# Ones multiplied into a free PSUM bank where TensorE waits, at 15 places of a two-block transformer kernel

## The chip, the cores and the metric

The kernel runs on one core of one Trainium2 chip. The metric is the device time of one execution in microseconds (us). TensorE (PE) does the matmuls, VectorE (DVE) and ScalarE (ACT) the elementwise work, and SyncE (SP) starts the DMA transfers that bring the weights. TensorE's clock has two levels, 1.2 and 2.4 GHz; the profile shows the granted clock as a share of 2.4 GHz, so 1.00 is the upper level and 0.50 the lower.

## The reference

All arrays are float32, with 256 tokens of width 1024. A first block has two layers, each an FFN, a token mixer and a second FFN, and each of the three is followed by a layer norm. A second block has one layer of multi-head latent attention (MLA) and one of gated linear attention (GLA), with a second stream of 256 context tokens.

```
def layer_norm(x, g, b):
    mu = jnp.mean(xf, -1, keepdims=True)
    var = jnp.mean(jnp.square(xf - mu), -1, keepdims=True)
    return ((xf - mu) * lax.rsqrt(var + LN_EPS) * g + b)
...
for l in range(2):                                   # first block
    y = swiglu(modulate(x, ...), ffn_w13[l, 0], ffn_w2[l, 0]);  x = layer_norm(ALPHA * x + 0.5 * (1 + ..) * y, ...)
    y = token_mixer(modulate(x, ...), w_in[l], ...);            x = layer_norm(ALPHA * x + (1 + ..) * y, ...)
    y = swiglu(modulate(x, ...), ffn_w13[l, 1], ffn_w2[l, 1]);  x = layer_norm(ALPHA * x + 0.5 * (1 + ..) * y, ...)
...
# in token_mixer, the gated delta rule:
qa, ka, va = jnp.split(causal_conv_silu(qkv_a, gdn_conv), 3, axis=-1)
qa = l2norm(split_heads(qa)); ka = l2norm(split_heads(ka))      # l2norm(x) = x * rsqrt(sum(x * x) + eps)
...
for i in range(2):                                   # second block: i = 0 MLA, i = 1 GLA
    hx = rms_norm(x, norm_g[i]) * (1 + scx) + sx
    hc = rms_norm(ctx, norm_g[i]) * (1 + scc) + sc
    yc, yx = mla_mixer(hc, hx, ...) if i == 0 else gla_mixer(hc, hx, ...)
```

## The kernel before, in words

Everything stays in SBUF except the weights, which arrive in chunks of 128x2048 float32 in a ring of 8 places. Activations lie with their width on the partitions, in 8 tiles of 128x256 (width by tokens). Most matmuls are made of three: weights and activations are split into a rounded high part and a remainder of type fp32r, and high by high, low by high and high by low are added up in PSUM. Those take 128x256 operands of type fp32r. ScalarE makes the high part of a chunk, VectorE the low part (`low`), both ahead of use. Each engine's program is written out by hand in one fixed order, with waits on the three semaphores `tensor_done`, `scalar_done` and `vector_done`; no scheduler moves anything.

The modules are numbered by `m`: in each layer an FFN (m = 0, 3), a mixer (1, 4), an FFN (2, 5), then MLA (6) and GLA (7). The places the change touches on TensorE:

- `norm_sums(m)`, run after each of the six modules 0 to 5. It sums over the 1024 channels by multiplying with a table of ones (a 128x128 left operand of plain float32): first the sums for the mean (`mu`, four matmuls into PSUM bank 4), then, once ScalarE has squared the centred values (`sq`) and VectorE has added some of them in pairs (`sqfold`), the sums of the squares (`var`, six matmuls into bank 5). After that ScalarE makes 1/sqrt, VectorE scales (`xn`), and the tiles of the next module's high part `xhi` come out, four from ScalarE and then four from VectorE, each of which releases two matmuls. Then follow the pass low by high, and the pass with the remainders `xlo` (`xl`), which VectorE makes from `xa` and `xhi`. For the norm of m = 5 the next module is MLA, which begins with the context's tiles (`whi_xa`).
- `mixer(l)`: TensorE projects the chunks `WIN_FIRST = [12, 0, 1, 2, 3, 4]` into banks 1 to 6. VectorE convolves each half chunk out of PSUM (`conv`, one TENSOR_SCALAR and three SCALAR_TENSOR_TENSOR) and ScalarE applies silu. After the fifth of them (i = 4) TensorE forms the sums of squares for q and k (`l2`, six 128x256 matmuls with the table `blk` into banks 1 to 3); it needs ScalarE's squares `l2sq`, which need the sixth half chunk convolved. ScalarE then computes the roots from these sums (`l2e`, `ri`), prepares a chunk (`win_high(m, 7)`), loads a table and copies the gates of chunk i = 5 (`proj_read_a`, res<-ps), for which VectorE waits before the ninth half chunk. Later TensorE multiplies k by k (`kk`), which waits for VectorE's `kb` and `gb_read`.
- the end of `mla()`: `next_sums(6)` adds the last squares for the next rms norm into bank 6 (`ms2`). Then `gla()` starts with `unit` number 0, which waits before each of its 8 tiles k for VectorE's `xd` and ScalarE's `xc`.

The matmul helper `mm` is line 347 for all of them, a transpose line 350; on ScalarE nearly everything is line 1459, on VectorE tensor_tensor is line 2068.

Of the kernel before, what the change touches and what calls it, by code (L numbers as in the profile page):

```python
# [90 lines left out]
def build(nc, stream, cond_in, cols_in, tab_in, wg_in, xt_in, ct_in, out, spread, marks):  # L91
# [3 lines left out]
    with ExitStack() as ctx:  # L95
# [52 lines left out]
        def step(*key):  # L148

            return marks[key][1] if marks else 1  # L150

        def step_of(*key):

            return (signals[marks[key][0]], marks[key][1]) if marks else (vector_done, 1)
# [17 lines left out]
        def bank(b, lo=0, hi=512):  # L172
            return PS[:, b, lo:hi]

        def banks(b, n):

            return PS[:, :, :].rearrange("p b n -> p (b n)")[:, b * 512:b * 512 + n]
# [4 lines left out]
        def table(name, lo=0, n=None):  # L182
            a, m = TAB[name]
            return tab[:, a + lo:a + lo + (m - lo if n is None else n)]
# [5 lines left out]
        def tiles(ap, n):  # L190
            return ap.rearrange("p (t n) -> p t n", n=n)
# [11 lines left out]
        ones = table("ones", 0, 128)  # L203
# [137 lines left out]
        def _(eng):  # L341
# [4 lines left out]
            def mm(o, l, r, start, stop, free=False):  # L346
                last[0] = nc.tensor.matmul(o, l, r, start=start, stop=stop, skip_group_check=free)  # L347

            def turn(o, i, k=128):
                last[0] = nc.tensor.transpose(o, i, ident[0:k, 0:k])  # L350

            def row_tile(parity):


                if parity:
                    last[0].then_inc(tensor_done, 1)
                    done.named()
                    eng.wait_ge(tensor_done, done.count)
# [17 lines left out]
            def release():  # L376

                last[0].then_inc(tensor_done, 1)
                done.named("chunk", held[0])
                if held[0] + 1 < len(order) and order[held[0] + 1] == ("rounded",):  # L380
                    found["chunk", held[0] + 1] = found["chunk", held[0]]
# [95 lines left out]
            def norm_sums(m):  # L477

                if m == 0:
                    eng.wait_ge(tables_in, 16)  # L480
                eng.wait_ge(vector_done, step("fold", m))
                for t in range(2):
                    mm(bank(4, 0, 256), ones, tiles(ff_sq, 256)[:, t], t == 0, False)
                for t in range(6, KT):
                    eng.wait_ge(vector_done, step("res", m, t))
                    mm(bank(4, 0, 256), ones, tiles(ff_res, 256)[:, t], False, t == KT - 1)
                last[0].then_inc(tensor_done, 1)
                done.named("mu", m)
                for t in range(4):
                    eng.wait_ge(scalar_done, step("sq", m, t // 2))  # L490
                    mm(bank(5, 0, 256), ones, tiles(ff_sq, 256)[:, t], t == 0, False)
                for q in range(2, 4):
                    eng.wait_ge(vector_done, step("sqfold", m, q))
                    mm(bank(5, 0, 256), ones, tiles(ff_sq, 256)[:, 2 * q], False, q == 3)
                last[0].then_inc(tensor_done, 1)
                done.named("var", m)

            def mixer(l):
                m = 3 * l + 1
# [16 lines left out]
                def project_halves(o, both, ch, t):  # L516

                    (hi, lo), at_t = both, slice(P * t, P * t + P)
                    for k in range(KT):
                        if ch < 13:  # L520
                            mm(o, hi[:, k, at_t], xhi[:, k, :], k == 0, False)
                            mm(o, lo[:, k, at_t], xhi[:, k, :], False, False)
                            mm(o, hi[:, k, at_t], xlo[:, k, :], False, k == KT - 1)
                        else:
                            mm(o, xhi[:, k, at_t], hi[:, k, :], k == 0, False)
                            mm(o, xhi[:, k, at_t], lo[:, k, :], False, False)
                            mm(o, xlo[:, k, at_t], hi[:, k, :], False, k == KT - 1)

                def project_first(both):

                    hi, lo = both
                    for k in range(KT):
                        eng.wait_ge(*step_of("xh", m, k))
                        for t in range(2):
                            mm(bank(1, 256 * t, 256 * t + 256), hi[:, k, P * t:P * t + P], xhi[:, k, :], k == 0 and t == 0, False, free=True)
                    eng.wait_ge(vector_done, step("wlow", m, 0))
                    for k in range(KT):
                        for t in range(2):
                            mm(bank(1, 256 * t, 256 * t + 256), lo[:, k, P * t:P * t + P], xhi[:, k, :], False, False, free=True)
                    for k in range(KT):  # L540
                        eng.wait_ge(vector_done, step("xl", m, k))
                        for t in range(2):
                            mm(bank(1, 256 * t, 256 * t + 256), hi[:, k, P * t:P * t + P], xlo[:, k, :], False, k == KT - 1, free=True)

                def weight_halves(i, ch):

                    no = take_both("win", l, ch)
                    if i:
                        eng.wait_ge(vector_done, step("wlow", m, i))
                    return tiles(low[:, (no + 1) % RING, :], 256), tiles(low[:, no % RING, :], 256)  # L550
# [88 lines left out]
                for i, ch in enumerate(WIN_FIRST):  # L639
                    both = weight_halves(i, ch)  # L640
                    if i == 0:
                        project_first(both)
                    else:
                        for t in range(2):
                            project_halves(bank(1 + i, 256 * t, 256 * t + 256), both, ch, t)
                    release()
                    found["proj", m, i] = found["chunk", held[0]]
                    if i == 4:
                        for p in range(3):
                            eng.wait_ge(*step_of("proj_read", m, p))  # L650
                        eng.wait_ge(scalar_done, step("l2sq", m))
                        for t in range(6):
                            mm(banks(1, 1536)[:, 256 * t:256 * t + 256], blk, tiles(g_sq, 256)[:, t], True, True)
                        last[0].then_inc(tensor_done, 1)
                        done.named("l2", m)
# [15 lines left out]
                for h in [0, 2, 4, 1, 3, 5]:  # L671
                    if h == 1:
                        row_tile(1)
                    for c in range(2):
                        u = 2 * h + c
                        mm(banks(1, 1536)[:, P * u:P * u + P], head(K, h, c), head(g_kb, h, c), True, True)
# [3 lines left out]
                for h in [0, 2, 4, 1, 3, 5]:  # L680
                    if h == 1:
                        row_tile(1)
                    for c in range(2):
                        u = 2 * h + c
                        mm(banks(4, 1536)[:, P * u:P * u + P], head(K, h, c), head(Q, h, c), True, True)
# [80 lines left out]
                for h in [0, 2, 4, 1, 3, 5]:  # L766
                    if h == 1:
                        row_tile(1)
                    mm(bank(3, 64 * h, 64 * h + 64), head(g_kg, h), head(S, h), True, True)
# [68 lines left out]
            def mla():  # L838
# [306 lines left out]
                next_sums(6)  # L1145
                last[0].then_inc(tensor_done, 1)
                done.named("ms2", 7)

            def gla():
                m = 7  # L1150
# [256 lines left out]
            for l in range(DEPTH):  # L1407
                ffn(l, 0)
                norm_sums(3 * l)
                mixer(l)  # L1410
                norm_sums(3 * l + 1)
                ffn(l, 1)
                norm_sums(3 * l + 2)
            mla()
            gla()

# [1604 lines left out]
```

## Time and profile before

| | |
|---|---|
| median of 3 runs | 1774.16 us (1772.45 to 1776.2) |
| the profiled execution | 1776.33 us, its span 1774.3 us |
| mean granted TensorE clock | 0.988 |
| PE busy | 1686.1 us (95%), 13112 instructions |
| DVE busy | 1323.5 us (75%) |
| ACT busy | 777.0 us (44%) |
| DMA | 331.92 MB, 48% of the 16 engines' span |

The span is the time from the first to the last instruction; 2.0 us of the execution lie around it. A plain float32 matmul shows as two MATMUL records, an fp32r matmul as one. In a timeline row, a start and a length are given for a merged run of alike instructions, xN is the number of records, and in brackets stands how long the engine was idle before it and which work ended that idle time. The records of PE overlap a little, since matmuls are pipelined: the price of one is best read from the distance of starts.

### The profile page before, as it was taken

What the parts mean: (1) busy time and instruction counts of PE and PEld (TensorE: products, weight loads), DVE (VectorE), ACT (ScalarE), POOL (GpSimd) and SP (SyncE); (2) the same over time, 40 slices, a digit from 0 to 9 for tenths busy, and PEclk for the clock granted to TensorE, in tenths of its full rate; (3) what the DMA queues carried; (4) which work ended last, traced back from release to release, by engine and by line L of the source; (5) the groups of instructions that cost most, each with busy time, mean ns of one, the idle gap of its engine ahead of it and who ended that gap; (6) DMA issues with size and microseconds to landing.
All of it is one profiled execution on the core that took longest, in us unless ns stands there. A gap on an engine that the chain in (4) does not pass through costs nothing. (4 is left out here: it accounts for less than half of the span.)

```text
span 1774.3 us, 30736 instructions
## 1 busy us (share of the span) xinstructions
PE 1686.1 (95%) x13112; PEld 1512.1 (85%) x13112; DVE 1323.5 (75%) x1965; ACT 777.0 (44%) x997; POOL 6.3 (0%) x14
## 2 busy tenths in 40 slices
PE   2999989999999999999899999999999999999998
PEld 2999978888899989999798779999886555759898
DVE  7777788855877778998878557999767768567844
ACT  2433365323633354343753327343652345355354
POOL 0000000000000000000000000000000000000000
PEclk9999999999999999999999999999999999999999
DMA  9868536351577746885364435776153200223102
GB/s 390 340 270 305 207 108 246 133 202 63 203 305 285 282 180 271 321 316 198 119 227 155 179 128 207 273 279 229 48 213 143 95 34 15 107 95 143 48 24 96
DMA packets 48807, 331.92 MB, mean 187 GB/s; under 512 B 5256, under 2 KB 8480, under 8 KB 9376
## 3 DMA queue, kind: packets, MB, share of 16 engines
q1 hardware_dynamic: 47808, 326.79, 48.2%
q0 software_dynamic: 864, 3.17, 0.7%
q8 instruction: 104, 1.70, 0.4%
q14 instruction: 31, 0.25, 0.0%
HBM read 328.87 MB, written 1.07 MB: 186 GB/s over the span
## 5 line engine op out<-in xcount | busy, mean ns | idle before, releaser
L347 PE MATMUL ps<-xhi,low 128*128 128x256 f32 x2048 | 499.5, 283 | 4.2 <-ACT xhi L1459 4.2
L347 PEld LDWEIGHTS ps<-xhi,low 128*128 128x128 f32 x2048 | 360.5, 190 | 6.4 <-ACT xhi L1459 5.6
L347 PE MATMUL ps<-xhi,whi_wk 128*128 128x256 f32 x1072 | 298.5, 288 | 40.5 <-ACT xhi L1459 38.7
L347 PE MATMUL ps<-xlo,whi_wk 128*128 128x256 f32 x1072 | 291.5, 281 | 0.0
L1459 ACT ACTIVATE wk<-ps 128x256 f32<-128x256 f32 (+5 forms) x219 | 108.1, 503 | 386.8 <-PE ps L347 320.8
L1459 ACT ACTIVATE whi_wk<-ring 128x2048 fp32r<-128x2048 f32 x100 | 191.6, 1918 | 195.3 <-DMA ring<-in_stream_dram 145.2
L347 PEld LDWEIGHTS ps<-xhi,whi_wk 128*128 128x128 f32 x1072 | 203.5, 195 | 43.2 <-issue 41.8
L2068 DVE TENSOR_TENSOR low<-ring,whi_wk 128x2048 fp32r<-128x2048 f32 (+1 forms) x101 | 228.4, 2264 | 6.6 <-ACT whi_wk L1459 6.6
L347 PE MATMUL ps<-wk 64*64 64x64 f32 (+10 forms) x2712 | 210.3, 262 | 5.8 <-ACT wk L1459 4.3
L347 PEld LDWEIGHTS ps<-wk 64*64 64x64 f32 (+4 forms) x2712 | 162.3, 146 | 55.0 <-issue 29.5
L347 PEld LDWEIGHTS ps<-xlo,whi_wk 128*128 128x128 f32 x1072 | 197.9, 189 | 0.0
L347 PE MATMUL ps<-hhi,low 128*128 128x256 f32 x704 | 196.8, 280 | 0.0
L2083 DVE CUSTOM_DVE_ANT_0 ring<-ring,cond,cols 128x1024 f32<-128x1024 f32 x144 | 178.3, 1278 | 11.0 <-DMA cols<-in_cols_dram 10.9
L1459 ACT ACTIVATE wk<-wk 128x256 f32<-128x256 f32 (+9 forms) x154 | 94.6, 643 | 200.9 <-DVE wk L2074 154.9
L347 PE MATMUL ps<-xa,ring 128*128 128x256 f32 (+1 forms) x608 | 146.0, 396 | 3.4 <-DVE xa L2071 3.1
L2068 DVE TENSOR_TENSOR wk<-wk,ps 128x256 f32<-128x256 f32 (+2 forms) x130 | 57.9, 462 | 122.1 <-ACT wk L1459 108.6
L347 PE MATMUL ps<-hhi,whi_wk 128*128 128x256 f32 x528 | 148.0, 280 | 0.0
L347 PE MATMUL ps<-hlo,whi_wk 128*128 128x256 f32 x528 | 147.9, 280 | 0.0
L347 PEld LDWEIGHTS ps<-xa,ring 128*128 128x128 f32 x608 | 114.3, 191 | 30.1 <-issue 11.5
L347 PEld LDWEIGHTS ps<-hhi,low 128*128 128x128 f32 x704 | 132.2, 188 | 0.0
L2068 DVE TENSOR_TENSOR low<-ring,low 128x2048 fp32r<-128x2048 f32 x41 | 93.2, 2286 | 48.4 <-ACT low L1459 48.2
L347 PE MATMUL ps<-wk,tab 128*128 128x256 f32 (+3 forms) x370 | 96.6, 422 | 22.8 <-ACT wk L1459 19.9
(141 smaller groups left out, 2861.7 us busy)
## 6 DMA issues: line engine op xcount, KB each, us to landing
ring<-in_stream_dram SPq DMA_DIRECT2D x302, 1024.0 KB, 5.7
ring<-in_cond_dram SPq DMA_DIRECT2D x4, 1024.0 KB, 4.6
wk<-spread_dram POOLq DMA_DIRECT2D x4, 384.0 KB, 5.1
wk<-spread_dram POOLq DMA_DIRECT2D x2, 768.0 KB, 6.9
tab<-in_tab_dram SPq DMA_DIRECT2D x1, 1440.0 KB, 20.5
res<-in_xt_dram SPq DMA_DIRECT2D x1, 1024.0 KB, 17.5
res<-in_ct_dram SPq DMA_DIRECT2D x1, 1024.0 KB, 9.9
out_dram<-wk SPq DMA_DIRECT2D x4, 256.0 KB, 2.4
```

The costliest lines, as they stand in the source:

```text
L347: last[0] = nc.tensor.matmul(o, l, r, start=start, stop=stop, skip_group_check=free)
L1459: return nc.scalar.activation(o, i, f, **kw)
L2068: return do(v.tensor_tensor(o, a, b, op), *key)
L2083: return do(v.tensor_tensor_reduce(o, w, c, 1.0, bias, MUL, ADD, total), *key)
```

## The change

A helper `idle(b, n)` issues n plain float32 matmuls of the table of ones (its first 128 columns the left operand, all 256 the right) into the first half of PSUM bank b, as one accumulation that nothing reads. It signals nothing and waits for nothing of its own. It is called with bank 0 everywhere:

- in `norm_sums`, 3 matmuls between the sums for the mean and those for the variance, and 4 after the latter: at six norms, 42 matmuls
- in `mixer`, 9 matmuls ahead of the sums of squares of q and k, behind the three waits for the banks (`proj_read` 0 to 2) and before the one for `l2sq`: in two mixers, 18
- at the end of `mla`, 6 matmuls after the last sums

Together these are 66 matmuls or 132 records, all on TensorE.

```
             def turn(o, i, k=128):
                 last[0] = nc.tensor.transpose(o, i, ident[0:k, 0:k])
+
+            def idle(b, n):
+
+                for i in range(n):
+                    mm(bank(b, 0, 256), ones, table("ones"), i == 0, i == n - 1)
...
                 last[0].then_inc(tensor_done, 1)
                 done.named("mu", m)
+                idle(0, 3)
                 for t in range(4):
                     eng.wait_ge(scalar_done, step("sq", m, t // 2))
...
                 last[0].then_inc(tensor_done, 1)
                 done.named("var", m)
+                idle(0, 4)
...
                         for p in range(3):
                             eng.wait_ge(*step_of("proj_read", m, p))
+                        idle(0, 9)
                         eng.wait_ge(scalar_done, step("l2sq", m))
...
                 next_sums(6)
                 last[0].then_inc(tensor_done, 1)
                 done.named("ms2", 7)
+                idle(0, 6)
```

The order of TensorE's instructions at a norm, that of m = 1 (before, and with + the new rows; `tab` holds the ones, `wk` the squares and sums, `xhi` the next module's tiles):

```order
 L347 MATMUL ps<-wk,tab 128x256
 L347 MATMUL ps<-wk,tab 128x256 [waits vector_done] x2
+L347 MATMUL ps<-tab 128x256 x3
 L347 MATMUL ps<-wk,tab 128x256 [waits scalar_done] x4
 L347 MATMUL ps<-wk,tab 128x256 [waits vector_done] x2
+L347 MATMUL ps<-tab 128x256 x4
 L347 MATMUL ps<-xhi,whi_wk 128x256 [waits scalar_done,chunk_landed_6]
 L347 MATMUL ps<-xhi,whi_wk 128x256
```

Three matmuls now stand ahead of the first one that waits for ScalarE's squares, and four ahead of the first one that waits for `xhi`; nothing else has another place.

And in the mixer of m = 1, at the sums of squares of q and k (`wk` with `tab`), between the projections (`xhi`, `xlo`):

```order
 L347 MATMUL ps<-xhi,low 128x256 x2
 L347 MATMUL ps<-xlo,low 128x256
-L347 MATMUL ps<-wk,tab 128x256 [waits vector_done,scalar_done]
+L347 MATMUL ps<-tab 128x256 [waits vector_done]
+L347 MATMUL ps<-tab 128x256 x8
+L347 MATMUL ps<-wk,tab 128x256 [waits scalar_done]
 L347 MATMUL ps<-wk,tab 128x256 x5
 L347 MATMUL ps<-xhi,low 128x256 [waits vector_done]
```

The wait for the PSUM banks has moved to the first of nine new matmuls; the wait for the squares stays where it was.

## Rows read from the trace of the kernel before

**Rows 1.** The page's busy times.
```profile
PE 1686.1 (95%) x13112; PEld 1512.1 (85%) x13112; DVE 1323.5 (75%) x1965; ACT 777.0 (44%) x997; POOL 6.3 (0%) x14
```

**Rows 2.** Stretches (start:end, length, busy by engine), ending in clock, DMA share, GB/s.
```profile
230.00:250.00 20.00, 17.89 (x130) 16.18 (x129) 14.70 (x31) 17.97 (x28) 0.00 (x0) 1.00 0.23 79
260.00:280.00 20.00, 14.76 (x94) 13.51 (x93) 18.77 (x33) 11.04 (x10) 3.12 (x5) 0.83 0.37 124
450.00:460.00 10.00, 9.05 (x59) 8.66 (x60) 9.89 (x22) 9.73 (x15) 0.00 (x0) 0.83 0.07 13
...
840.00:860.00 20.00, 16.45 (x106) 15.04 (x105) 14.26 (x32) 15.90 (x25) 0.00 (x0) 0.91 0.14 54
1260.00:1280.00 20.00, 17.98 (x103) 15.54 (x103) 11.34 (x18) 13.42 (x28) 0.00 (x0) 0.91 0.00 1
1570.00:1580.00 10.00, 7.99 (x16) 3.60 (x17) 7.49 (x16) 7.20 (x12) 0.00 (x0) 0.83 0.46 193
```

**Rows 3.** Timeline, TensorE, the norm of m = 0 and what follows.
```profile
228.76 2.95 PE L347 MATMUL ps<-wk,tab 128*128 128x256 f32 x12 [1.45 <-ACT wk L1459]
233.82 5.32 PE L347 MATMUL ps<-xhi,low 128*128 128x256 f32 x32 [2.11 <-ACT xhi L1459]
241.31 0.40 PE L347 MATMUL ps<-xhi,low 128*128 128x256 f32 x2
```

**Rows 4.** Timeline, TensorE, after the norms of m = 3, 1 and 4.
```profile
847.98 5.67 PE L347 MATMUL ps<-xhi,low 128*128 128x256 f32 x32 [2.11 <-ACT xhi L1459]
855.48 0.40 PE L347 MATMUL ps<-xhi,low 128*128 128x256 f32 x2
...
450.94 3.94 PE L347 MATMUL ps<-xhi,whi_wk 128*128 128x256 f32 x16 [2.20 <-ACT xhi L1459]
458.76 0.28 PE L347 MATMUL ps<-xhi,whi_wk 128*128 128x256 f32 x1
...
1065.17 3.94 PE L347 MATMUL ps<-xhi,whi_wk 128*128 128x256 f32 x16 [2.20 <-ACT xhi L1459]
1073.11 0.28 PE L347 MATMUL ps<-xhi,whi_wk 128*128 128x256 f32 x1
```

**Rows 5.** Timeline, TensorE, the start of MLA, after the norm of m = 5.
```profile
1263.03 1.89 PE L347 MATMUL ps<-whi_xa,low 128*128 128x256 f32 x8 [1.22 <-ACT whi_xa L1459]
1265.72 9.23 PE L347 MATMUL ps<-whi_xa,low 128*128 128x256 f32 x56 [0.80 <-ACT whi_xa L1459]
1274.78 3.62 PE L347 MATMUL ps<-wk,tab 128*128 128x256 f32 x16
1278.05 4.17 PE L347 MATMUL ps<-whi_xa,low 128*128 128x256 f32 x32
```

**Rows 6.** Timeline, TensorE and ScalarE, sums of squares in the mixer m = 1.
```profile
269.32 5.38 PE L347 MATMUL ps<-wk,tab 128*128 128x256 f32 x12 [5.24 <-ACT wk L1459]
274.22 0.72 PE L347 MATMUL ps<-xhi,low 128*128 128x256 f32 x2
...
274.74 1.55 ACT L1459 ACTIVATE wk<-ps,cols 128x1536 f32<-128x1536 f32 x1 [4.26 <-PE ps L347]
```

**Rows 7.** Timeline, VectorE: the wait for the gates in m = 1, `gb_read`, then m = 4.
```profile
281.40 0.48 DVE L2071 TENSOR_SCALAR wk<-ps,cols 128x256 f32<-128x256 f32 x1 [0.86 <-ACT res L1459]
289.93 1.76 DVE L2068 TENSOR_TENSOR wk<-wk,tab 128x1536 f32<-128x1536 f32 x1
...
895.64 0.48 DVE L2071 TENSOR_SCALAR wk<-ps,cols 128x256 f32<-128x256 f32 x1 [0.59 <-ACT res L1459]
```

**Rows 8.** Timeline, TensorE, the first matmuls of `kk` in the mixer m = 1.
```profile
291.87 5.92 PE L347 MATMUL ps<-wk 64*128 64x128 f32 x48
```

**Rows 9.** Timeline, TensorE and VectorE, the start of GLA.
```profile
1572.01 10.28 PE L347 MATMUL ps<-xa,ring 128*128 128x512 f32 x20 [3.14 <-DVE xa L2071]
...
1577.05 0.73 DVE L2071 TENSOR_SCALAR xa<-wk,aux,mod 128x256 f32<-128x256 f32 x2
```

**Rows 10.** Timeline, VectorE, a low half in the projections of MLA.
```profile
1327.19 2.29 DVE L2068 TENSOR_TENSOR low<-ring,low 128x2048 fp32r<-128x2048 f32 x1 [4.03 <-ACT low L1459]
```

More of the change, by code:

```diff
@@ L350, in turn, with idle @@
                 last[0] = nc.tensor.transpose(o, i, ident[0:k, 0:k])
+            def idle(b, n):
+                for i in range(n):
+                    mm(bank(b, 0, 256), ones, table("ones"), i == 0, i == n - 1)
             def row_tile(parity):
@@ L488, in norm_sums @@
                 done.named("mu", m)
+                idle(0, 3)
                 for t in range(4):
@@ L496, in norm_sums @@
                 done.named("var", m)
+                idle(0, 4)
             def mixer(l):
@@ L650, in mixer @@
                             eng.wait_ge(*step_of("proj_read", m, p))
+                        idle(0, 9)
                         eng.wait_ge(scalar_done, step("l2sq", m))
@@ L1147, in mla @@
                 done.named("ms2", 7)
+                idle(0, 6)
             def gla():
```

## The prediction

> **What bounds the kernel now.** I read the page first: TensorE is busy for 95% of the span, VectorE for 75%, ScalarE for 44% [rows 1]. So the time is TensorE's, apart from the few places where it waits; whatever slows its matmuls or makes it wait is on the path. Next I read the granted clock by stretches. It is 1.00 nearly everywhere. It falls at nine places, the first of which, before 60 us, lies ahead of every edit. The other eight each follow a wait of TensorE of over a microsecond: behind the norms of m = 1 to 5, at the squares' sums of both mixers and at the start of GLA (five of them stand in [rows 2]). The clock's mean gives their length: 260 to 280 us at 0.83 is 20 x 0.17 / 0.5 = 6.8 us at the lower level, 1.2 GHz, and the second mixer is alike. 450 to 460, 840 to 860, 1260 to 1280 and 1570 to 1580 us give 3.4 to 3.6 us each, and the norms of m = 2 and 4 are alike. Behind the norm of m = 0 the clock stayed at 1.00 [rows 2], although it has the same waits, 1.45 us ahead of the squares' sums and 2.11 us ahead of `xhi` [rows 3]. Waits of this size are thus close to the edge: the same pattern sometimes drops the clock and sometimes doesn't.
>
> **The price of an added matmul.** In [rows 5] eight plain 128x256 matmuls (16 records) take 1278.05 - 1274.78 = 3.27 us at full clock, 0.41 each. In [rows 6] six of them (12 records) take 274.22 - 269.32 = 4.90 us at half clock, 0.82 each. So the added groups take 3 x 0.41 = 1.23, 4 x 0.41 = 1.64, 9 x 0.41 = 3.7 and 6 x 0.41 = 2.5 us. The waits they are put into are 1.45 and 2.11 us in the norms, 5.24 in the mixer and 3.14 ahead of GLA [rows 3, 6, 9]: each group fits and ends 0.2 to 1.5 us before the awaited work is there. The exception is the norm of m = 5, whose second wait is 1.22 us [rows 5] against a group of 1.64: `whi_xa` starts 0.4 us late. But these first 8 matmuls are released tile by tile by ScalarE, and behind them the engine stands idle for another 0.80 us [rows 5], which takes the delay up. In the mixer the group first waits for the PSUM banks; VectorE convolves two more half chunks and ScalarE squares 1536 columns between the release of bank 3 and the end of the wait, so the release falls near the wait's beginning. I cost the 66 matmuls at nothing. Without this cover they would cost 66 x 0.41 = 27 us.
>
> They keep TensorE occupied for most of each wait, so I expect the clock at 1.00 at all eight places. What is that worth at each?
>
> **Norms of m = 3, 1, 2 and 4.** Behind m = 3 the clock fell, behind m = 0 it didn't, and the work behind them is the same. From the first `xhi` matmul to the first one of the next chunk it is 241.31 - 233.82 = 7.49 us without the fall and 855.48 - 847.98 = 7.50 us with it [rows 3, 4]. It cost nothing: these matmuls are released tile by tile, and the slower clock hides in the gaps. Behind m = 1 and 4 the distance is 7.82 and 7.94 us [rows 4], so it cost 0.33 and 0.45; for m = 2 I take their mean, 0.4. Together 1.2 us, bounds 0 and 4 x 1.7. What is late next is VectorE's `xlo`.
>
> By the Trainium skill (TensorE: Matmul & The Clock Gate, section "Terms") the penalty of a throttled clock is the throttled time times (1 - K/N), here half of it. By that each of these would be worth 1.7 us, and the four 6.8. The twin norms, m = 0 and 3, speak against it with 0.01 us.
>
> **Norm of m = 5.** Here the low stretch lies in a run of matmuls that after its start waits for nobody: 56 records from 1265.72 to 1274.78, 9.06 us [rows 5]. 32 of the same kind at full clock take 4.17 us with a tail of 0.28 [rows 4, 5], so 0.125 each, and 56 take 7.0. Of the 2.06 us over, some 0.4 are the release by ScalarE at the start, and 1.7 are half of the 3.4 us at half clock. All of it is on the path. What waits behind: the low halves of MLA's weights come from VectorE; the one at 1327.19 (which waited 4.03 us for ScalarE and, through it, for the chunk) is done at 1329.48 [rows 10], and TensorE takes it at about 1331, an estimate from the units of 5.6 us before it. That leaves some 1.8 us of room, just enough. I take 1.7, bounds 0 and 1.7.
>
> **Mixers, m = 1 and 4.** At full clock the six matmuls take 2.45 instead of 4.90 us. TensorE is ready that much earlier, but what counts is `kk`. It started at 291.87, 0.18 us after VectorE had finished `gb_read` at 289.93 + 1.76 = 291.69 [rows 7, 8]. So VectorE sets this point, and it gains only as much of its own waiting as hangs on TensorE: the 0.86 us for ScalarE's copy of the gates [rows 7], which stands behind the root computation that had waited 4.26 us for the six matmuls [rows 6]. ScalarE comes 2.45 us earlier, so the 0.86 go whole. In m = 4 this wait is 0.59 us [rows 7]. I take 0.86 + 0.59 = 1.45 us, bounds 0 and 2 x 2.6 (the 2.45 and what the two matmuls at 274.22 lose at half clock).
>
> **Start of GLA.** `unit` 0 and the first two tiles of unit 1 are 10 matmuls of 512 columns, 20 records, 10.28 us from 1572.01 [rows 9]. At full clock one takes 2 x 0.41 = 0.82 us, all ten 8.2. But VectorE delivers the 8 tiles only until 1577.78 [rows 9], one per 0.93 us with the last two closer together. That puts the end of the eighth at about 1577.42 + 2 x 0.82 = 1579.06 and of the tenth at 1580.7, against 1572.01 + 10.28 - 0.2 of tail = 1582.1. I take 1.4, bounds 0 and 1.7.
>
> **Sum.** 1.2 + 1.7 + 1.45 + 1.4 = 5.75 us. Against the profiled execution that is 1776.33 - 5.75 = 1770.6; taken off the median of the runs, 1774.16, it is 1768.4. The profiled one lay 2.2 us above the median, and since the clock falls behind one norm and not behind its twin, part of the runs' spread of 3.75 us may be where the falls lie, so the median run may have less to win than the profiled one. I lean to the median and add 0.6 for that: 1769.0.
>
> **Rivals.**
> 1. *A part is swallowed.* The norm of m = 5 is the largest term and rests on 0.1 us of room; if MLA's weights don't come earlier with TensorE, it gives 0. So might GLA's start, if VectorE's next products set the pace. Left are 1.2 + 1.45 = 2.65 us: 1771.5. For it: MLA's low halves wait for the weights [rows 10]. Against it: a chunk's place in the ring is freed by TensorE, and so earlier.
> 2. *More was on the path than I count.* The eight low stretches are 2 x 6.8 + 6 x 3.4 = 34 us and half is 17: 1757 if all counted, which the twin norms exclude. The mixers at 5.2 instead of 1.45 make 9.5 us: 1764.7. The skill's rule named above, taken for the whole kernel, is the first of these.
> 3. *Slower: the norms' groups run past the wait.* At 0.82 us a matmul, as at half clock, three take 2.46 against a wait of 1.45 us and four 3.28 against 2.11 [rows 3]: 1.0 + 1.2 us at each of six norms, 13 us, against 3 that the rest still gains: 1784. It decides from 0.48 us a matmul. For it: the drop may already come in the first wait. Against it: the squares' sums on both sides of these waits ran at full clock.
> 4. *The clock falls all the same*, since these matmuls don't hold it or since 0.2 to 1.5 us of each wait stay open: 1774. Against it: in the mixer the clock came back while nothing but six such matmuls ran [rows 2, 6].
>
> **Chances.** Forecast (1767 to 1771) 0.52; rival 1 0.20; rival 2 0.12, nearly all of it at its part; rival 3 0.06; rival 4 0.10. What a measurement of this kernel can tell from no change is about 0.2%, 3.5 us, so faster means below 1770.6. That takes nine tenths of the forecast, rival 2 and little of rival 1: 0.60. Within 0.2% are the rest of the first two and rival 4: 0.34. Slower 0.06. The range leaves out rival 3, the far end of rival 2 and the worst of rival 4: 1764.6 to 1774.3.
>
> **What would show it.** In the changed kernel's profile the clock is 1.00 at all eight places and lower only before 60 us. The ones' records begin right behind `mu` and `var` and leave 0.2 to 0.5 us of waiting. The six sums of squares take 2.45 us, VectorE's wait for res is gone in both mixers, and TensorE waits for VectorE ahead of `kk`, which comes 0.9 us earlier against the start of its mixer. From `xhi` to the next chunk it is 7.4 to 7.5 us behind five norms. MLA's run of 56 takes 7.4 instead of 9.06 us, GLA's first 20 records 8.8 instead of 10.28. The prediction is wrong if the clock still falls at a norm, if `kk` comes 2.5 us earlier, or if the term of m = 5 is gone again by 1370 us.

## The result, and the profile after

| | before | changed kernel |
|---|---|---|
| median | 1775.02 us (1772.45 to 1776.2, 7 runs) | 1785.39 us (1778.75 to 1789.11, 7 runs) |
| ratio | | 1.0053, 95% interval 1.0041 to 1.0066 |
| profiled execution | 1776.33 us, span 1774.3 us | 1778.75 us, span 1776.8 us |
| mean granted clock | 0.988 | 0.994 |

The change makes the kernel 0.5% slower, though the mean clock rose. The profiled execution is the fastest of the seven runs. The page of the changed kernel shows TensorE busier by 24 us (66 matmuls at 0.41 us are 27; matmuls that ran at another clock than before are in this figure too), and VectorE and ScalarE as before [rows 1]:

```profile
PE 1710.1 (96%) x13244; PEld 1531.1 (86%) x13244; DVE 1323.4 (74%) x1965; ACT 777.1 (44%) x997; POOL 6.3 (0%) x14
```

The stretches (start:end, length, busy by engine; clock, DMA share and GB/s last) answer to [rows 2]:

```profile
260.00:280.00 20.00, 18.75 (x137) 17.62 (x136) 18.59 (x34) 12.34 (x12) 3.12 (x5) 1.00 0.35 113
280.00:300.00 20.00, 15.10 (x97) 14.23 (x96) 13.78 (x16) 9.59 (x23) 0.00 (x0) 0.80 0.95 357
300.00:310.00 10.00, 9.94 (x50) 9.42 (x50) 6.27 (x8) 0.39 (x1) 0.00 (x0) 0.56 0.01 2
450.00:460.00 10.00, 9.38 (x43) 7.32 (x41) 6.55 (x17) 4.74 (x9) 0.00 (x0) 1.00 0.76 311
840.00:860.00 20.00, 18.44 (x112) 15.63 (x111) 16.70 (x36) 9.15 (x15) 0.00 (x0) 1.00 0.15 54
1260.00:1280.00 20.00, 18.67 (x112) 15.89 (x111) 14.31 (x25) 13.88 (x27) 0.00 (x0) 1.00 0.15 53
1570.00:1580.00 10.00, 9.45 (x29) 4.77 (x27) 8.09 (x14) 6.17 (x9) 0.00 (x0) 1.00 0.79 316
```

All eight places stand at 1.00 now. But from 280 to 310 us, in the first mixer, where the kernel before ran at 1.00, the clock is 0.80 and then 0.56. Taken microsecond by microsecond it is at its lower level twice: for 3.4 us from 285.0 us on and for 13.7 us from 295.2 us on. What happens there is read from VectorE's timeline (start, length, work, and in brackets the idle time ahead and what ended it):

```profile
283.46 1.76 DVE L2077 TENSOR_TENSOR wk<-wk 128x1536 f32<-128x1536 f32 x1
285.32 0.42 DVE L2086 COPY wk<-ps 128x256 f32<-128x256 f32 x1
286.83 0.17 DVE L2086 COPY small<-wk 128x3 f32<-128x3 f32 x1 [1.08 <-DMA wk<-spread_dram]
286.91 1.82 DVE L2077 TENSOR_TENSOR wk<-wk 128x768 f32<-128x768 f32 x2
292.16 1.76 DVE L2077 TENSOR_TENSOR wk<-wk,tab 128x1536 f32<-128x1536 f32 x1 [3.44 <-DMA wk<-spread_dram]
```

and TensorE's:

```profile
267.67 2.86 PE L347 MATMUL ps<-wk,tab 128*128 128x256 f32 x12 [1.25 <-ACT wk L1468]
270.18 0.58 PE L347 MATMUL ps<-xhi,low 128*128 128x256 f32 x2
...
283.73 0.50 PE L347 MATMUL ps<-xhi,low 128*128 128x256 f32 x2 [1.91 <-ACT wk L1468]
...
294.07 9.67 PE L347 MATMUL ps<-wk 64*128 64x128 f32 x48 [2.93 <-DVE wk L2077]
```

The last row of VectorE is `gb_read`. Here, and at the copy before it, VectorE waits 3.44 and 1.08 us for `wk<-spread_dram`: three small loads on GpSimd's queue that spread the gates over the partitions. The kernel before has no such wait. TensorE then stands idle for 2.93 us ahead of `kk` (the last row), and the 48 records of `kk` take 9.67 us where they took 5.92 [rows 8], because the clock is at its lower level for the 13.7 us.

The third row of TensorE is a second new wait: its projections, 4.4 us ahead of before by now, stand still for 1.91 us until ScalarE is done, and behind that comes the short low stretch. In this execution it costs nothing, since TensorE waits ahead of `kk` anyway. The same wait is there in the second mixer (1.91 us ahead of 906.58 us), where the clock stayed up in this execution; other executions show what it can cost there (experiments 7 to 9).

Why are the loads late? The DMA issues of GpSimd and SyncE, first of the kernel before, then of the changed one (start and length of the group of issues):

```profile
276.83 1.35 POOL L2850 DMA_DIRECT2D wk<-spread_dram  x2 [1.34 <-DMA spread_dram<-wk]
278.18 0.58 POOL L2853 DMA_DIRECT2D wk<-spread_dram  x1
...
280.38 6.46 SPq L1432 DMA_DIRECT2D ring<-in_stream_dram  x4
```
```profile
275.29 1.36 POOL L2859 DMA_DIRECT2D wk<-spread_dram  x2 [1.35 <-DMA spread_dram<-wk]
276.63 0.58 POOL L2862 DMA_DIRECT2D wk<-spread_dram  x1
...
276.00 6.25 SPq L1441 DMA_DIRECT2D ring<-in_stream_dram  x4
```

The spread loads start 1.5 us earlier, by as much as this trace is ahead from 89 us on. No edit lies there: in this execution the clock didn't fall at 42 us, as it had in the profiled one of before. The ring's transfers start 4.4 us earlier. Those wait for the place of a chunk to be freed by TensorE's projections, which stand behind the squares' sums. The sums start 1.65 us earlier (267.67 against 269.32) and the projections behind them 4.04 (270.18 against 274.22), since six matmuls at full clock take 2.4 us less; the last 0.3 us come in the projections. The transfers had come 2.2 us after the last spread load; now they come ahead of it. The transfers' times from issue to landing (last column, median), of the kernel before from its page and of the changed one between 262 and 312 us:

```profile
wk<-spread_dram POOLq DMA_DIRECT2D x2, 768.0 KB, 6.9
```
```profile
wk<-spread_dram POOLq DMA_DIRECT2D x2, 384.0 KB, 8.3
wk<-spread_dram POOLq DMA_DIRECT2D x1, 768.0 KB, 15.5
```

6.9 us became 15.5. By the Trainium skill (DMA: Bandwidth & Descriptors, section "Queues, rings and completion order") each DMA engine takes the queues that have work for it in turn, a packet at a time. The longer times beside transfers of another queue fit that; the taking of turns itself no view here shows.

In sum, the start of the same VectorE instruction in both traces, counted from the span's start:

| place | before | after | difference | what lies between |
|---|---|---|---|---|
| wait for the gates, m = 1 | 281.40 | 279.12 | -2.28 | 1.5 from before 89 us; 0.7 gained: the wait of 0.86 is gone |
| `gb_read`, m = 1 | 289.93 | 292.16 | +2.23 | 4.5 lost by the spread loads |
| behind `kk` and its like | 307.01 | 315.40 | +8.39 | 6.2 lost by the low clock |
| behind the norm of m = 1 | 504.61 | 512.56 | +7.95 | 0.4 gained |
| FFN of m = 3 | 691.44 | 696.07 | +4.63 | 3.3, no gain of the change (below) |
| end of the FFN of m = 3 | 810.65 | 817.42 | +6.77 | 2.1 lost again (below) |
| second mixer, gates | 895.64 | 901.97 | +6.33 | 0.4 gained: the wait of 0.59 |
| MLA | 1279.40 | 1284.09 | +4.69 | 0.4 lost at `gb_read`, m = 4; 2.0 gained at the norms of m = 4 and 5 |
| GLA | 1580.62 | 1584.23 | +3.61 | 1.1 gained |
| the whole execution | | | +2.42 | 1.2 between 1580 and 1700 us, no gain of the change (below) |

At 691 us VectorE of the kernel before waits 6.89 us, since ScalarE had waited 9.40 us for one of the ring's chunks; the changed kernel's waits 3.6 us. But kernels 2, 3, 6, 7 and 8 below gain 2.3 to 2.8 us at the same place, with and without ones at the norms, and 3, 13 and 6, the last of them without any ones, lose 1.6, 1.6 and 1.9 us of it again by 810 us, as this one loses 2.1. So that chunk came late in the one profiled execution of before, and the 3.3 and the 2.1 are not the change's. Nor are the 1.5 us ahead of 89 us: the clock falls at 42 us in four of the seventeen profiled executions (before, 5, 7 and 14), and the other thirteen are 1.4 to 1.6 us ahead of before there, kernels without ones among them. Nor the last 1.2 us: kernel 10, which has no ones, gains them too.

### The profile page after: what moved, and what is told of

Same layout as the page of the kernel before. It is cut to its first block and busy times, and to the rows that moved or that the text cites. A ratio compares the mean times of both kernels' runs of the same rounds, so it can differ in the third digit from the quotient of the medians.

```text
span 1776.8 us, 30998 instructions
## 1 busy us (share of the span) xinstructions
PE 1710.1 (96%) x13244; PEld 1531.1 (86%) x13244; DVE 1323.4 (74%) x1965; ACT 777.1 (44%) x997; POOL 6.3 (0%) x14
## 5 line engine op out<-in xcount | busy, mean ns | idle before, releaser
L347 PE MATMUL ps<-wk 64*64 64x64 f32 (+10 forms) x2712 | 214.0, 264 | 9.3 <-ACT wk L1468 4.3
L347 PE MATMUL ps<-whi_xa,low 128*128 128x256 f32 (+1 forms) x552 | 114.0, 327 | 0.8 <-ACT whi_xa L1468 0.8
## 6 DMA issues: line engine op xcount, KB each, us to landing
wk<-spread_dram POOLq DMA_DIRECT2D x2, 768.0 KB, 13.7
tab<-in_tab_dram SPq DMA_DIRECT2D x1, 1440.0 KB, 20.5
```

## The experiments

All ratios are to the kernel before, run beside on the same chip, with the 95% interval.

**1. Without the mixers' ones.**
```
-                        idle(0, 9)
                         eng.wait_ge(scalar_done, step("l2sq", m))
```


> The changed kernel without the nine ones matmuls of the mixers; the ones in the norms and ahead of GLA stay. Theory A (collision): the loss comes from the mixers alone. There the squares' sums end 2.5 us earlier, the ring transfers behind them start earlier and fall on the spread loads, for which VectorE then waits. Without them the kernel is faster than before by what the norms and GLA give, 3 to 4.5 us: about 1771 us, with no wait for spread_dram. Theory B (the added matmuls cost by themselves, 66 x 0.2 us or more): about three quarters of the loss stays, 1782 us. Theory C (the clock's low stretch at the mixer's kk comes wherever it wants once the others are gone): loss stays, about 1780.

Measured: 0.9978 [0.9968, 0.9987], 1773.13 us, 4.1 us below before on the same chip. No wait for the spread loads. The norms and GLA gain what they were to gain (1.2 + 1.7 + 1.4 = 4.3 us by the prediction); the loss is the mixers'.

**2. The mixers' ones only** (`idle(0, 3)`, `idle(0, 4)` and `idle(0, 6)` taken out).

> Before, with the nine ones matmuls of the two mixers alone. Theory A: all of the loss and none of the gain, 1775 + 10 + 4 = 1785 to 1790 us; VectorE waits for spread_dram ahead of gb_read by 3 us or more in at least one mixer. Theory B: 18 of the 66 matmuls, so 3 us of loss: 1778. Theory C: about 1780.

Measured: 1.0048 [1.0033, 1.0062]. VectorE waits 0.90 and 3.19 us for the spread loads, `kk` takes 10.73 us behind an idle time of 3.98:
```profile
286.70 0.17 DVE L2083 COPY small<-wk 128x3 f32<-128x3 f32 x1 [0.90 <-DMA wk<-spread_dram]
...
291.79 1.76 DVE L2074 TENSOR_TENSOR wk<-wk,tab 128x1536 f32<-128x1536 f32 x1 [3.19 <-DMA wk<-spread_dram]
```

**3. The changed kernel, with the ring's transfers held** until the spread loads have landed. This takes the meeting away and leaves every one of the 66 matmuls.
```
+            held_back = set()
...
+                for l in range(DEPTH):
+                    if n - 1 <= RING + found["chunk_no", "win", l, WIN_FIRST[5]][1] <= n and l not in held_back:
+                        held_back.add(l)
+                        eng.wait_ge(decays_in, 16 * (l + 1))
```


> The changed kernel, with SyncE holding back the ring transfers that the release of the sixth projected chunk lets go until the third spread load of that mixer has landed. Theory A: nothing runs beside the spread loads, VectorE does not wait for them, kk is not late and the clock stays up: faster than before by 3 to 6 us, 1769 to 1772. If the ring then runs short of weights, a wait for a chunk shows in the mixer and some of it is lost. Theories B and C: no change against the changed kernel, 1785.

Measured: 0.9962 [0.9949, 0.9975], 1769.53 us. Its timelines, TensorE and VectorE, and its transfers (768 KB again in 7.0 us):
```profile
289.67 5.92 PE L347 MATMUL ps<-wk 64*128 64x128 f32 x48
...
285.75 0.16 DVE L2091 COPY small<-wk 128x3 f32<-128x3 f32 x1
...
287.74 1.76 DVE L2082 TENSOR_TENSOR wk<-wk,tab 128x1536 f32<-128x1536 f32 x1
```
```profile
wk<-spread_dram POOLq DMA_DIRECT2D x2, 384.0 KB, 5.2
wk<-spread_dram POOLq DMA_DIRECT2D x1, 768.0 KB, 7.0
```
```profile
280.00:300.00 20.00, 18.21 (x153) 17.34 (x152) 18.34 (x22) 9.87 (x24) 0.00 (x0) 1.00 0.90 352
300.00:310.00 10.00, 10.00 (x138) 8.63 (x136) 4.08 (x7) 4.82 (x11) 0.00 (x0) 1.00 0.58 227
```
No wait, the clock at 1.00, and `gb_read` 2.19 us ahead of before instead of 2.23 behind. This version beats both kernels.

**4 and 5. Ones ahead of `kk`, against the low clock alone.** Seven, then twelve, into bank 4; the wait for the loads stays.
```
                 fill(2)
+                idle(4, 7)
                 eng.wait_ge(vector_done, step("kb", m))
```


> The changed kernel with seven more ones matmuls (2.9 us) into the free bank 4 ahead of the two waits before kk in each mixer. It leaves the collision and takes away the idle time that it makes on TensorE. If the low clock of 13.7 us at kk follows from that idle time, the clock stays at 1.00 there and about 6 us of the 10 come back: 1779. If the small matmuls of kk and qk (64 rows) lower it by themselves, the stretch stays and the time is 1785 or more.

> As e4_kk_ones, with twelve ones matmuls (4.9 us) instead of seven ahead of kk. In e4 the seven ended 2.1 us before kk could start and the clock fell 1.7 us into kk. If idle time ahead of kk is what lowers the clock, twelve leave no gap in the first mixer and the low stretch there is gone; the collision's 4.5 us stay: about 1775 if the second mixer has as long a wait, and somewhat more, to 1778, if twelve run past the wait there. If kk and qk lower the clock themselves, a low stretch of 10 us stays in the first mixer and the time is 1780 or more.

Measured: 1.0018 [1.0006, 1.003] and 1.0043 [1.0029, 1.0057]. TensorE with seven, then with twelve in the first and in the second mixer:
```profile
289.27 3.18 PE L347 MATMUL ps<-tab 128*128 128x256 f32 x14
294.54 9.41 PE L347 MATMUL ps<-wk 64*128 64x128 f32 x48 [2.09 <-DVE wk L2078]
```
```profile
291.11 5.34 PE L347 MATMUL ps<-tab 128*128 128x256 f32 x24
296.38 5.92 PE L347 MATMUL ps<-wk 64*128 64x128 f32 x48
...
908.70 5.34 PE L347 MATMUL ps<-tab 128*128 128x256 f32 x24
913.98 5.92 PE L347 MATMUL ps<-wk 64*128 64x128 f32 x48
```
Seven end 2.1 us ahead of `kk` and the clock falls all the same, for 10.2 instead of 13.7 us. With twelve it stays, `kk` takes 5.92 us, and from `gb_read` to behind `kk` 1.5 us are lost instead of 6.2. So the two parts of the loss are separate. The 1.5 are the price of the fill: twelve end 1.4 us after `gb_read` is done (293.15 + 1.76 = 294.91, against 296.3). In the second mixer they end 4.0 us after it (909.98 against 913.98), where the wait they were to fill is 1.46 us long, and they cost 4.8 us; the seven cost 2.6 there. That is why 5 missed its 1775 to 1778 us. It is the prediction's third rival, at a place where the change has no ones.

**6. The hold alone, on the kernel before.**

> The kernel before with nothing but the hold of e3 on SyncE, no ones at all. Theory A: in before, the ring transfers start only 1.6 us after the last spread load is issued and VectorE does not wait for the spread loads, so the hold has nothing to mend: 1777, no difference, and e3's gain is the ones'. Rival: the hold by itself gives the gain (less contention for the spread loads or the ring): 1770 to 1773.

Measured: 1.0002 [0.9992, 1.0011]. The hold is worth nothing by itself; in 3 it removes what the ones bring about.

**7. The nine ones in the second mixer only** (`if l:` ahead of `idle(0, 9)`).

> The changed kernel with the mixers' nine ones in the second mixer alone. Theory A, with the collision tied to how closely the ring transfers follow the spread loads: the second mixer's wait for the spread loads was 0.55 us in the changed kernel's trace against 4.5 in the first, so most of the loss goes: 1772 to 1775. If both mixers lose alike, half the loss stays: 1779.

Measured: 0.9974 [0.9964, 0.9983]. The second mixer's ones cost nothing that the ratio shows against kernel 1 (0.9978); the first one's do. The profile shows a gain and a loss there: 0.4 us at the wait for the gates, and 1.5 us by 921 us, behind the wait of 1.91 us for ScalarE in the projections (from 899.4 us on the clock is low for 3.4 us) and a wait of 0.88 us for the spread loads.

**8. As 3, with the norms' ones at m = 5 only.**

> e3 with the norms' ones only at m = 5 (those of m = 0 to 4 left out). By the prediction's terms the clock falls again behind the norms of m = 1 to 4, at 0.3 to 0.45 us each and nothing at m = 3: 1.2 us slower than e3, 1770.7. If each low stretch costs half its length, 5 us or more slower. If these norms' ones cost time themselves, faster than e3.

Measured: 0.9998 [0.9988, 1.0008], 5 to 6 us worse than 3, not 1.2. In the profiled runs 1.4 us have come by 802 us, which is near the size of the term. 1.6 more come by 925 us: in the second mixer the clock fell at 897.7 us for 3.4 us, in the projections ahead of `kk`, behind the wait for ScalarE that the mixer's ones open. `kk` itself ran at full clock, but later, for TensorE had no wait left ahead of it to hide the stretch:
```profile
897.51 0.68 PE L347 MATMUL ps<-xhi,low 128*128 128x256 f32 x2 [1.91 <-ACT wk L1475]
...
904.88 5.92 PE L347 MATMUL ps<-wk 64*128 64x128 f32 x48
```
The norm of m = 4 adds 0.4, and the one of m = 5 adds 1.5, where the clock fell although the ones were there:
```profile
1260.33 1.89 PE L347 MATMUL ps<-tab 128*128 128x256 f32 x8
1261.87 1.73 PE L347 MATMUL ps<-whi_xa,low 128*128 128x256 f32 x8
1264.40 9.23 PE L347 MATMUL ps<-whi_xa,low 128*128 128x256 f32 x56 [0.80 <-ACT whi_xa L1475]
```
9.23 us again [rows 5]. A filled wait doesn't promise the clock: behind the same fill and the same wait of 0.80 us it fell in this execution and not in that of the changed kernel. It is no rare case. Of the thirteen profiled executions with ones at m = 5 the clock fell there in six (kernels 1, 5, 8, 12, 13 and 15). The last 1.5 us come behind the norms. How much of the 5 to 6 us is owed to the norms' ones stays open.

**9. The changed kernel again**, on another chip.

> The changed kernel once more, for a second trace: its first trace was of its fastest run (1778.75 against a median of 1785). Theory A: the part missing from the first trace is the same mechanism in the second mixer, whose wait for the spread loads was only 0.55 us there: now a wait of some us for spread_dram and a low stretch at kk near 910 us. If the trace is again at 1779 with nothing there, or the rest lies elsewhere (norms, MLA), that part of the theory falls.

Measured: 1.0038 [1.0022, 1.0055], 1779.37 to 1790.85 us. VectorE waits 0.99 and 3.21 us for the spread loads, and 1.54 us in the second mixer; `kk` of the first takes 10.74 us. The place is the same. In the second mixer the clock is low for 3.4 us from 907.8 us on, in the projections ahead of `kk`, and `kk` runs at full clock; 1.5 us are lost there between 902 and 921 us, where the first trace lost 0.4. That is part of what was looked for, not the 6 us between the profiled runs and the median.

**10. The meeting without any ones**: on the kernel before, GpSimd issues the spread loads only when the sixth projection has freed its chunk.
```
                 eng.wait_ge(rows_stored, 32 * (l + 1))
+                eng.wait_ge(*step_of("proj", m, 5))
```


> The kernel before, no ones at all, with the two pair loads on GpSimd's queue waiting until TensorE has finished the sixth projected chunk, so that they start together with the ring transfers that the same event lets go (about 3 us later than before). Theory A: the meeting of the two is what costs, so VectorE waits for spread_dram in both mixers, TensorE stands idle ahead of kk, the clock falls at kk, and the time is 1777 + 2 x (5 to 10) = 1787 to 1797. If the ones are needed for the loss, it is 1777 to 1779.

Measured: 1.0148 [1.0128, 1.0169], 1805.43 us, more than the 1787 to 1797 expected. The loads start only 1.7 us later than before, but next to the ring's (278.57 and 278.03 us), and take 10.2 and 15.4 us:
```profile
wk<-spread_dram POOLq DMA_DIRECT2D x2, 384.0 KB, 10.2
wk<-spread_dram POOLq DMA_DIRECT2D x1, 768.0 KB, 15.4
```
```profile
290.05 0.17 DVE L2082 COPY small<-wk 128x3 f32<-128x3 f32 x1 [4.23 <-DMA wk<-spread_dram]
...
295.35 1.76 DVE L2073 TENSOR_TENSOR wk<-wk,tab 128x1536 f32<-128x1536 f32 x1 [3.41 <-DMA wk<-spread_dram]
```
It is the same wait, the same idle TensorE and the same fall of the clock (0.80, then 0.50 from 300 to 310 us), in both mixers, without one added matmul.

**11. As 3, without GLA's ones.**

> e3 without the six ones matmuls ahead of GLA. The prediction's term for them was 1.4 us, the changed kernel's trace showed 1.1 less of lead there: 1.1 to 1.4 us slower than e3 and a low stretch near 1565 us. If the other drops come back with it through a shift, more.

Measured: 0.9976 [0.9965, 0.9988]. The clock fell again at GLA's start and its first 20 records took 11.72 us instead of 9.20. That puts it 2.5 us behind kernel 3 there; before had taken 10.28 us at this place, with a low stretch half as long. The ratios don't size GLA's ones: the intervals of 3 and 11 overlap, and kernel 12, which is 3 again on the same chip as 11, came out slower than 11.

**12. Kernel 3 again.**

> The kernel of e3 again, on the same chip as the changed kernel, e10 and e11. It should repeat 0.996 of before, 1769 to 1771 us, and be 15 us faster than the changed kernel.

Measured: 0.9974 [0.9962, 0.9986]. The gain holds, a little smaller. In its profile 3.3 us of it went at 1000 us (last section) and 1.5 at the norm of m = 5, where the clock fell behind the ones. It is 11 us faster than kernel 9 on the same chip, not 15.

**13 to 15. Which mixer?** The median of the changed kernel lies 6 us above its profiled runs (1778.75 and 1779.58 us), and those show nearly all of the loss in the first mixer. Held in the first mixer only (`for l in (0,)` in 3), held in the second only (`for l in (1,)`), and the nine ones in the first only (`if l == 0:`):

> The changed kernel with the ring's transfers held behind the spread loads in the first mixer only. If the whole loss is made in the first mixer, this is as good as holding in both: ratio 0.996 to 0.998 of before, and runs within 5 us of each other. If most runs of the changed kernel lose another 5 to 6 us in the second mixer, where the profiled runs showed only 0.6 to 1.5 us of waiting for the spread loads, that part stays: 0.999 to 1.002, with a spread of 8 us or more. The trace has no wait of VectorE for the spread loads at 283 to 292 us, and 0.5 to 1.5 us of it near 910 us.

> The changed kernel with the transfers held in the second mixer only. Loss all in the first mixer: the same as the changed kernel, 1.003 to 1.006. Half of it in the second: 1.000 to 1.002, and runs that lie closer together than the 11 us of the changed kernel. Trace: VectorE waits 1 and 3.4 us for the spread loads near 287 and 292 us, the clock is low for 13.7 us behind it, and nothing of this at 910 us.

> The changed kernel without the nine matmuls of the second mixer (the norms' and GLA's stay). If the runs' spread of 11 us comes from the second mixer, this kernel's runs lie within 5 us and its median near 1780, ratio 1.000 to 1.003. If it comes from the first mixer or from elsewhere, it is like the changed kernel, 1.003 to 1.006, with the same spread. The mirror image, the nine in the second mixer only, was 0.9974.

Measured: 0.9957 [0.9943, 0.9971] (1769.61 us); 1.002 [1.0012, 1.0029]; 1.004 [1.0027, 1.0053]. Held in the first alone is as good as in both, though VectorE waits 0.62 us for the loads in the second. So what the changed kernel loses against before comes from the meeting in the first mixer, for the median run too. The hold there is worth more than the profiles explain: from 1.0053 or 1.0038 (9) to 0.9957 it is 14 to 17 us, and the traces put 10 to 11 us in this place. The second has a smaller part at most: the hold there brought 1.002, the upper edge of what half of the loss in the second was to give, an interval that overlaps that of 9 and not that of the first comparison, 1.0041 to 1.0066. The five runs of 15 lie within 4 us of each other, so whether the 11 us of the changed kernel need the second mixer is not settled.

## Why the prediction was wrong

The forecast was 1769.0 us and 0.60 for faster; the median is 1785.39. The range ended at 1774.3.

**The step that failed is the mixers' term**: "I take 0.86 + 0.59 = 1.45 us, bounds 0 and 2 x 2.6." The mechanism named there took place: the sums of squares ran at full clock, and the waits for the gates were gone in both mixers, 0.7 and 0.4 us. What failed is the lower bound of 0. The text said that "TensorE is ready that much earlier, but what counts is `kk`", and followed only the next instruction that needs TensorE. It didn't follow the chunks that TensorE frees. They let SyncE's transfers start 4.4 us earlier, ahead of the last spread load, and `gb_read`, which the same paragraph named as what sets `kk`, needs those loads. The term measured in the first mixer: +0.7, then -4.5 (VectorE's waits) and -6.2 (low clock in `kk` and behind it), so -10 us instead of +0.86. Kernel 3, which takes away only the meeting, and kernel 10, which makes it without ones, show it as the cause; 7 and 13 show the place. The same look at one instruction alone missed a smaller thing: a TensorE that is 2.4 us earlier must wait for ScalarE in its own projections (1.7 to 1.9 us), a new wait that nothing fills. In six profiled executions (the changed kernel in the first mixer; 2, 7, 8, 9 and 11 in the second) the clock fell behind it for 3.4 us, and each of the five executions with it in the second mixer lost 1.5 us there, 8 and 11 among them, whose loads are held.

**"The clock at 1.00 at all eight places"** held in both profiles of the changed kernel. Over the profiles of all kernels it held where the ones stand in twelve executions each behind the norms of m = 1 to 4, at the first mixer's squares and at GLA. It held in ten of twelve at the second mixer's squares (not in 3 and 4) and in seven of thirteen at m = 5. So at m = 5 the profiles of the changed kernel were also lucky: what the prediction named as a sign of being wrong, "if the clock still falls at a norm", shows in the other six. That elsewhere the clock would be "lower only before 60 us" did not hold: new waits in the mixers dropped it. (At the very end, from 1769.5 us on in before, it falls in every profile; the prediction's nine places leave that out.)

**Norms of m = 3, 1, 2 and 4**, 1.2 us. From `xhi` to the next chunk it is 7.50 us at m = 0, 7.49 at m = 3, 7.40 at m = 1, 7.41 at m = 2 and 7.41 at m = 4 (7.4 to 7.5 forecast). On VectorE, 0.4 us of that show behind m = 1 and 0.5 behind m = 4, and nothing behind m = 2 and m = 3: about 1.0 us. The rows behind m = 1 answer to [rows 4]:
```profile
459.32 3.34 PE L347 MATMUL ps<-xhi,whi_wk 128*128 128x256 f32 x16 [0.47 <-ACT xhi L1468]
...
466.72 0.28 PE L347 MATMUL ps<-xhi,whi_wk 128*128 128x256 f32 x1
```
The matmuls of 0.41 us fit into the waits and left 0.15 and 0.38 to 0.47 us, so the third rival, that the groups run past the wait, didn't come about there.

**Norm of m = 5**, 1.7 us. A little smaller, and only where the clock holds: the 56 records take 1279.47 - 1271.91 = 7.56 us against 9.06 [rows 5], forecast 7.4. Norms 4 and 5 together gave 2.0 us of 2.15, still there at 1580 us.
```profile
1269.38 1.73 PE L347 MATMUL ps<-whi_xa,low 128*128 128x256 f32 x8
1271.91 7.72 PE L347 MATMUL ps<-whi_xa,low 128*128 128x256 f32 x56 [0.80 <-ACT whi_xa L1468]
1279.47 3.62 PE L347 MATMUL ps<-wk,tab 128*128 128x256 f32 x16
```

**Start of GLA**, 1.4 us: 1.1 measured; the 20 records took 9.20 us against 10.28 [rows 9], forecast 8.8. Against kernel 11, where the clock was low for 6.8 us there and not for 3.4, it is 2.5.
```profile
1573.40 2.75 PE L347 MATMUL ps<-tab 128*128 128x256 f32 x12
1576.70 9.20 PE L347 MATMUL ps<-xa,ring 128*128 128x512 f32 x20 [0.55 <-DVE xa L2080]
```

**The sum**, 5.75 us. Where the meeting is taken away the kernel gains 0.43% and 0.38% (13 and 3), that is 7.6 and 6.8 us of 1777, or 4.6 in 12. In the changed kernel's profile the gains named by the prediction come to 4.7 us (1.1 in the mixers, 1.0, 1.5, 1.1). The sum without the mixer's loss was of the right size.

**The rivals.** The price of a low clock by the rule of the Trainium skill (TensorE: Matmul & The Clock Gate, section "Terms": about the throttled time times (1 - K/N), here half of it) was set aside with the twin norms' 0.01 us. In `kk` and behind it the low stretch of 13.7 us cost 6.2, against 6.85 by the rule, and at 1000 us (last section) 6.8 us cost 3.3, against 3.4. Both readings fit their place: where the matmuls are released one by one the slower clock hid in the gaps, where they stood dense it was paid. The fourth rival, that the clock falls all the same, came true in part, at m = 5 and at the second mixer's squares as told above. The only rival on the slower side, 0.06, was a direct price of the added matmuls; the loss came by another way.

**What stays open.** Over the seven runs of the changed kernel the mean clock goes from 0.994 to 0.990 while the span goes from 1776.8 to 1787.0 us. That is (1 - 0.990) x 2 x 1787.0 = 35.7 us at the lower level against 21.3, so 14.4 more for 10.2 us. Kernel 13 has 0.998 or 0.999 in all five runs, which lie within 2.1 us. So the slower runs have more of the low clock, enough for the time they lose. Where it falls in them no trace shows, for both traces of the changed kernel are of its quicker runs (1778.75 and 1779.58 us). Other kernels show three places where it can: the norm of m = 5 and the projections of the second mixer, at 1.5 us each, and the stretch of the last section, at 3.3. Together that would be the 6 us between profile and median; that it is so is not shown.

## What to carry to other kernels

When a stage ends earlier, list everything that its end releases, the places it frees in a ring of transfers above all, and look at what those transfers will then meet; a bound of zero on a gain needs a reason for each. Matmuls that fill a wait can keep the clock only at that wait, and not in every execution; here the ones that ended 2.1 us ahead of `kk` didn't, and sized for one place they cost wherever the wait is shorter. So look at more than one profile before a fill is called good. A mean clock that rises says nothing of the time: here it rose from 0.988 to 0.994 while the kernel became slower. What a low stretch costs depends on what runs under it: next to nothing where the matmuls wait for other engines anyway, and about half its length where they follow each other without a gap.

## What the runs showed of the hardware

- **A small load beside large ones.** 768 KB on GpSimd's queue took 6.9 us when 1 MB transfers on SyncE's queue were issued 2.2 us behind it, and 15.5 us when from 0.6 us ahead of it; 384 KB took 8.3 instead of 5.1. Held apart it was 7.0 and 5.2 again. In the second mixer of the changed kernel 768 KB took 11.9 us, and VectorE waited 0.55 us for it.
- **The clock can fall with TensorE busy.** In the second mixer of kernels 1, 12, 14 and 15, from 1000.6, 1000.1, 1011.5 and 1010.2 us, and at the same place of the first mixer in kernel 6 (387.6 us), which has no ones, the clock is at its lower level for 6.8 us while the longest wait of the engine in the 25 us ahead is 0.06 us. It is busy for 10.00 us of 10, with runs of small matmuls (64x64, 64x256, 128x64). Kernel 12, and its twin 13 at the same place without the fall:
```profile
1000.00:1010.00 10.00, 10.00 (x55) 7.64 (x54) 5.11 (x10) 0.80 (x2) 0.00 (x0) 0.66 0.00 0
...
1001.02 4.14 PE L347 MATMUL ps<-wk 128*128 128x64 f32 x20
```
```profile
1000.96 2.25 PE L347 MATMUL ps<-wk 128*128 128x64 f32 x20
```
  VectorE fell back by 3.2 to 3.3 us there in each of the five. The same program does it in some executions and not in others (kernel 12 and not kernel 3), so it is a source of spread between runs.
- **It can stay low with TensorE busy, too.** Under `kk` and what follows it was low for 13.7 us, with 9.94 us busy of the 10 from 300 us on. In kernel 10 it was low for 20.5 us, of which 5.3 lie in the idle time ahead of `kk`.
